# A decoder layer on one core: twelve expert slots move from the last merge and output into the samples' stage, and VectorE adds some of them there

## The chip, the cores and the metric

The kernel runs on one core of a Trainium2 chip. The metric is the device time of one execution in microseconds. Three runs gave 3580.25, 3585.42 and 3592.96, a median of 3585.42 us.

## What is computed

One layer of a decoder trunk for 1024 prompt tokens and 8 samples of one token each, all in float32:

```
xn = rmsnorm(x);  z = xn @ w_in                     # heads of three branches, and gates
merged = sig(ga)*(attention @ w_br_a) + sig(gb)*(pooling @ w_br_b) + sig(gc)*(mlstm @ w_br_c)
x = x + merged @ w_out
x = x + peer(rmsnorm(x))       # 8 heads, top 16 of 128*128 experts each
peer: sum over 8*16 experts e of  softmax_gate(e) * gelu(xn . u[e]) * v[e]
```

The samples use the same weights, with a cache of 128 keys and values, 15 rows of pooling history, and an mLSTM state of 32 matrices of 128 x 128 that is read, used and written back.

## The kernel before, in words

The prompt is eight tiles of 128 tokens. A pass handles two tiles; there are four passes (0 to 3), and the last one also carries the samples. A pass has these stages: norm (`n0`), input projection (`z`), branches (`b`), in the last pass alone the samples' own branches (`x`), merge (`m`: 24 units, each a gate product of 16 matmuls at L1105 and a branch product of 8 at L1109), output (`o`: 8 units, L1126), norm (`n1`), queries (`g`), and the experts' search (`f`, `search`, `e`).

The experts' work of each tile is cut into 128 **slots**. A slot stands for one expert of each of a tile's 128 tokens. There are 1032 of them: 8 x 128, and 8 for the samples. A slot is

- a gather of 128 rows of 8 KB (u and v beside each other) by GpSimd, L1982, into one of 8 places of a ring (place n % 8). It is issued when the place's earlier slot n-8 has been added (`free`);
- a dot product on VectorE, L1515, of the u half with x;
- a gelu (per pair of slots), a weight and a diagonal matrix on ScalarE (L1211, L1223, L1230);
- the adding of weight times the v half to the tile's sum: either on TensorE, four matmuls against the diagonal at L894, or, for the slots in `ON_DVE`, on VectorE at L1475, with no diagonal.

The slots of pass p's tiles are worked off during the stages of pass p+1 and, for the last pass, in the end of the program. `SHARES` says how many slots fall into each stage. `share_out` spreads them over the stage's **points**, named places in the program of each engine. At a point VectorE does the point's dots; TensorE adds only the slots up to the point's first, so it is one point behind. `ON_VECTOR` says which places of the ring VectorE adds itself, by stage; never the first 16 slots of a tile or its last.

The samples' stage has nine points, x0 to x8 (`sample_tensor` L431 on, `sample_scalar`, `sample_vector`). In it tile 4 ends: at x1 VectorE takes its sum out of PSUM (L1487), and TensorE may add slot 640, the first of tile 5, only after that. On VectorE the stage has small operations (L568 to L640), four rounds of the mLSTM state (`state_round`, five operations on 128 x 1024 each, L557 to L563: round 0 before x3, round 1 before x4, round 2 before x5, round 3 before x6), and the end (`c_h2`, `c_y`), which lies between x6 and x8. On TensorE, `fill` (L426, L427) brings a round's rows into PSUM: fill 0 before x3, fill 1 before x4, fill 2 before x5, fill 3 before x6. The first merge unit waits for `c_y`.

In the merge, the weights of unit k+2 (768 KB) are requested by SyncE when unit k's branch product is done (L770), since two buffers take turns; the output's (512 KB) likewise.

Of the kernel before, what the change touches and what calls it, by code (L numbers as in the profile page):

```python
# [34 lines left out]
LAST = PASSES - 1  # L35
# [27 lines left out]
RING = 8  # L63
# [10 lines left out]
def share_out():  # L74


    points = {
        "n0": [("n", 0)], "z": [("z", c, t) for c in range(NZ) for t in range(NT)],
        "b": [("b", t, i) for t in range(NT) for i in range(BRANCH_POINTS)], "x": [("x", i) for i in range(SAMPLE_POINTS)],
        "m": [("m", k, i) for k in range(3 * KC) for i in range(2)], "o": [("o", i) for i in range(NO)], "n1": [("n", 1)],  # L80
        "g": [("g", i) for i in range(3)], "f": [("f", h, i) for h in range(PH) for i in range(4)],
        "late": [("f", h, i) for h in range(2, PH) for i in range(4)],
        "search": [("e", i) for i in range(SEARCH_POINTS)], "e": [("e", i) for i in range(SEARCH_POINTS, TAIL_POINTS)],
    }
    plan = [{} for _ in range(PASSES)]
    done = 0
    for p, shares in enumerate(SHARES):
        at = done
        for stage, share in shares:
            for key in points[stage]:  # L90
                at += share / len(points[stage])
                to = 2 * round(at / 2)
                plan[p][key] = (done, to)
                done = to
    assert done == SLOTS
    return plan
# [4 lines left out]
    (("late", 40),),  # L101
# [3 lines left out]
)  # L105
SOON = (4, 4, 4, 4)
PLAN = share_out()
ON_VECTOR = {"z": (3, 7), (LAST, "z"): (1, 3, 5, 7), "b": (1, 5), "m": (1, 4, 6), (LAST, "m"): (1, 3, 5, 7), "o": tuple(range(RING)), "f": (2,)}


def vector_slots():

    own = set()
    for p, of_pass in enumerate(PLAN):
        for key, (first, last) in of_pass.items():
            for n in range(first, last):
                if n % RING in ON_VECTOR.get((p, key[0]), ON_VECTOR.get(key[0], ())) and PK <= n % P < P - 1:
                    own.add(n)
# [1969 lines left out]
```

## Time and profile before

| what | value |
|---|---|
| median of three runs | 3585.42 us |
| profiled execution, its own time | 3589.58 us |
| its span, first to last instruction | 3587.8 us |
| mean granted TensorE clock | 0.947 |
| TensorE busy | 3073.4 us (86%) |
| VectorE busy | 2324.5 us (65%) |
| ScalarE busy | 1083.9 us (30%) |
| GpSimd busy | 1216.1 us (34%) |
| moved by DMA | 1313.33 MB, mean 366 GB/s |

A time in a row is in microseconds from the span's start. A granted clock of 1.00 is 2.4 GHz, 0.50 is 1.2 GHz, and a value between is a mixture of both in that stretch. DMA share is the mean busy share of the 16 DMA engines; it can come out a little above 1. In the timeline, brackets hold the idle time before an instruction and what ended it.

### The profile page before, as it was taken

Reading aid. Unit: us, or ns where it says so; the run is one execution under the profiler, and the core shown is the slowest. Engines: PE = TensorE matmul, PEld = TensorE weight load, DVE = VectorE, ACT = ScalarE, POOL = GpSimd, SP = SyncE. Lnnn points to the kernel's source line nnn. Section 1 sums busy time; section 2 is a strip of 40 time slices with the busy share of each in tenths; the row PEclk is TensorE's granted clock in tenths of the full one; section 3 lists DMA queues with packets and bytes.
Section 4 is the critical chain, followed back from the end, with each engine's and each line's share of the span. In section 5 each row is a group of like instructions: output and inputs, shape, how many; then the busy total and the mean of one; then the engine's idle time right before and its main releaser. Section 6 shows DMA issues by size and latency. Waiting matters only on the chain.

```text
span 3587.8 us, 31309 instructions
## 1 busy us (share of the span) xinstructions
PE 3073.4 (86%) x9822; PEld 1776.0 (50%) x9822; DVE 2324.5 (65%) x5255; ACT 1083.9 (30%) x3269; POOL 1216.1 (34%) x1043
## 2 busy tenths in 40 slices
PE   7988789989987889988987989988998787777777
PEld 4667544546665544445665544443566453322222
DVE  1331678785666678885566778886667768864444
ACT  1221243442212333442222333343221234332222
POOL 0100233343343233442333333342334324444342
PEclk9999899999998999989998989997999899999999
DMA  5344899999999889999999989998999989999998
GB/s 166 102 126 140 328 386 398 382 401 364 420 420 386 352 349 421 417 372 372 417 420 401 413 349 408 390 386 318 397 420 419 404 339 401 421 420 421 422 421 354
DMA packets 206565, 1313.33 MB, mean 366 GB/s; under 512 B 27170, under 2 KB 29290, under 8 KB 73751
## 3 DMA queue, kind: packets, MB, share of 16 engines
q0 software_dynamic: 152800, 1084.63, 74.3%
q1 hardware_dynamic: 49111, 213.07, 15.5%
q10 hardware_dynamic: 4488, 13.63, 1.1%
q8 instruction: 78, 1.28, 0.1%
q14 instruction: 88, 0.72, 0.1%
HBM read 1294.81 MB, written 17.61 MB: 366 GB/s over the span
## 4 chain that ended last, share of the span: by engine, by line
PE 54%; DMA 29%; DVE 9%; ACT 4%; issue 3%; POOL 1%; ACTq 0%; DVEq 0%; POOLq 0%; SPq 0%
PE ps L894 23%; DMA arena<-uv,eidx 21%; PE ps L930 10%; PE ps L1143 5%; PE ps L1105 5%; DVE arena L1515 4%; DMA wbuf<-w_merge 4%; PE ps L1109 3%; PE ps L1126 2%; DMA wbuf<-w_o 2%; DMA xx<-xs_scr 1%; DVE xx L1475 1%; ACT wgt L1223 1%; PE ps L948 1%; PE ps L911 1%
## 5 line engine op out<-in xcount | busy, mean ns | idle before, releaser
L1982 POOL DMA_INDIRECT arena<-uv,eidx x1032 | 1200.4, 1163 | 2188.3 <-PE ps L894 1633.7
L894 PE MATMUL ps<-arena,dgs 128*128 128x512 f32 x3196 | 1542.4, 625 | 289.7 <-ACT dgs L1230 257.4
L1515 DVE CUSTOM_DVE_ANT_0 arena<-arena,xx 128x1024 f32<-128x1024 f32 x1024 | 1238.5, 1222 | 663.2 <-DMA arena<-uv,eidx 614.6
L894 PEld LDWEIGHTS ps<-arena,dgs 128*128 128x128 f32 x3196 | 614.5, 199 | 1041.8 <-issue 621.1
L1211 ACT ACTIVATE gel<-dots 128x2 f32<-128x2 f32 x516 | 104.3, 202 | 1423.4 <-DVE dots L1515 1422.7
L930 PE MATMUL ps<-wbuf,xT 128*128 128x420 f32 (+1 forms) x1152 | 426.8, 520 | 13.5 <-DMA wbuf<-w_z 12.6
L1475 DVE SCALAR_TENSOR_TENSOR xx<-arena,wgt,xx 128x1024 f32<-128x1024 f32 x225 | 288.3, 1282 | 60.1 <-ACT wgt L1223 57.5
L1105 PE MATMUL ps<-xT,wbuf 128*128 128x256 f32 (+1 forms) x1344 | 314.8, 388 | 11.9 <-DMA wbuf<-w_merge 10.1
L930 PEld LDWEIGHTS ps<-wbuf,xT 128*128 128x128 f32 (+1 forms) x1152 | 204.6, 180 | 235.6 <-issue 220.8
L1105 PEld LDWEIGHTS ps<-xT,wbuf 128*128 128x128 f32 x1344 | 258.0, 193 | 79.4 <-DMA wbuf<-w_merge 26.0
L1230 ACT ACTIVATE dgs<-cst,wgt 128x128 f32<-128x128 f32 x799 | 286.9, 396 | 15.9
L1223 ACT ACTIVATE wgt<-gates,gel 128x1 f32<-128x1 f32 x1032 | 247.7, 287 | 23.0 <-ACT gel L1211 2.6
L1143 PE MATMUL ps<-xT,wbuf 128*128 128x256 f32 (+1 forms) x1024 | 233.3, 383 | 6.3 <-issue 6.3
L1143 PEld LDWEIGHTS ps<-xT,wbuf 128*128 128x128 f32 x1024 | 195.6, 191 | 55.7 <-issue 28.8
L1109 PE MATMUL ps<-yT,wbuf 128*128 128x256 f32 (+1 forms) x768 | 182.6, 382 | 6.1 <-DMA wbuf<-w_merge 5.3
L1126 PE MATMUL ps<-wbuf,R 128*128 128x256 f32 (+1 forms) x576 | 144.8, 411 | 41.8 <-DMA wbuf<-w_o 35.5
L1109 PEld LDWEIGHTS ps<-yT,wbuf 128*128 128x128 f32 x768 | 145.2, 190 | 52.9 <-issue 26.3
L1126 PEld LDWEIGHTS ps<-wbuf,R 128*128 128x128 f32 (+1 forms) x576 | 109.5, 195 | 78.3 <-DMA wbuf<-w_o 44.3
L1766 DVE SCALAR_TENSOR_TENSOR T<-T,ps 128x256 f32<-128x256 f32 (+1 forms) x96 | 40.4, 420 | 122.2 <-PE ps L1109 121.2
L1280 ACT ACTIVATE arena<-ps 128x420 f32<-128x420 f32 x64 | 33.3, 520 | 250.3 <-PE ps L930 250.2
L911 PE MATMUL ps<-cst,R 128*128 128x128 f32 x128 | 29.3, 423 | 90.1 <-DVE R L1538 90.1
L1404 ACT ACTIVATE yT<-ps 128x256 f32<-128x256 f32 x64 | 24.4, 382 | 221.4 <-PE ps L1143 221.4
(366 smaller groups left out, 1993.1 us busy)
## 6 DMA issues: line engine op xcount, KB each, us to landing
wbuf<-w_merge SPq DMA_DIRECT2D x84, 768.0 KB, 8.5
wbuf<-w_z SPq DMA_DIRECT2D x64, 840.0 KB, 8.8
wbuf<-w_q SPq DMA_DIRECT2D x64, 512.0 KB, 7.9
arena<-uv,eidx POOLq DMA_INDIRECT x1032, 12.5
wbuf<-w_o SPq DMA_DIRECT2D x32, 512.0 KB, 7.9
xin<-x_prompt SPq DMA_DIRECT2D x8, 1024.0 KB, 11.7
wbuf<-w_merge SPq DMA_DIRECT2D x12, 512.0 KB, 8.3
grow<-gains SPq DMA_DIRECT2D x8, 512.0 KB, 9.8
```

Source lines behind the costliest of these rows:

```text
L894: done = mm(ps[:, half, :], dgs[:, j, :], ring[:, j, row_], start=(q == 0), stop=(q == P - 1), skip_group_check=True)
L930: last = mm(ps[0:rows_, 2 + 2 * (pair % 2) + t if t < NT else 6 + pair % 2, 0:ZP], xT[:, HALF * half + kc, t * P:t * P + rows_], wv[:, kc, :],
L1105: last = mm(ps[:, 2 + 2 * b, m], wv[:, c, :], xT[:, c, m], start=(c == 0), stop=(c == KC - 1))
L1109: last = mm(ps[:, 3 + 2 * b, m], wv[:, 8 + c, :], yT[:, 4 * b + c, m], start=(c == 0), stop=(c == 3))
L1126: last = mm(ps[0:rows_, 2 + 2 * (b % 2) + t if t < NT else 6 + b % 2, 0:OC], mT[:, HALF * half + c, t * P:t * P + rows_], wv[:, c, :], sta ...
L1143: last = mm(ps[:, 2 + k, m], wv[:, c, :], xT[:, c, m], start=(c == 0), stop=(c == KC - 1))
L1211: f(gel[:, j:j + 2], dots[:, j:j + 2], ACT.Gelu).then_inc(s["gelud"], 1)
L1223: last = f(wgt[:, j + i:j + i + 1], gate_of(n + i), ACT.Copy, scale=gel[:, j + i:j + i + 1])
L1230: f(dgs[:, j + i, :], ident, ACT.Copy, scale=wgt[:, j + i:j + i + 1]).then_inc(s["diagd"], 1)
L1475: v.scalar_tensor_tensor(xres, ring[:, j, D:2 * D], wgt[:, j:j + 1], xres, ALU.mult, ALU.add).then_inc(free[j], 1)
L1515: v.tensor_tensor_reduce(ring[:, j, 0:D], ring[:, j, 0:D], x, 1.0, 0.0, ALU.mult, ALU.add, dots[:, j:j + 1]).then_inc(s["dotted"], 1)
L1982: g.indirect_dma_start(ring[:, j, :], None, uv, bass.IndirectOffsetOnAxis(ap=experts, axis=0)).then_inc(got[j], 16)
```

## The change

In the last pass the samples' stage gets 36 slots where it had 24, the merge 52 where it had 60, the output 16 where it had 20. In the samples' stage VectorE adds the slots in ring places 1, 3, 5 and 7.

```diff
-    (("n0", 4), ("z", 62), ("b", 46), ("x", 24), ("m", 60), ("o", 20), ("n1", 4), ("g", 6), ("f", 46), ("search", 80), ("e", 152)),
+    (("n0", 4), ("z", 62), ("b", 46), ("x", 36), ("m", 52), ("o", 16), ("n1", 4), ("g", 6), ("f", 46), ("search", 80), ("e", 152)),
 )
-ON_VECTOR = {"z": (3, 7), (LAST, "z"): (1, 3, 5, 7), "b": (1, 5), "m": (1, 4, 6), (LAST, "m"): (1, 3, 5, 7), "o": tuple(range(RING)), "f": (2,)}
+ON_VECTOR = {"z": (3, 7), (LAST, "z"): (1, 3, 5, 7), "b": (1, 5), "m": (1, 4, 6), (LAST, "m"): (1, 3, 5, 7), "o": tuple(range(RING)), "f": (2,), "x": (1, 3, 5, 7)}
```

`share_out` turns this into the following plan. The samples' stage ran from slot 640 to 663, with 2, 4, 2, 2, 4, 2, 2, 4, 2 dots at x0 to x8; it now runs from 640 to 675 with four at every point. The merge has slots 676 to 727 (it had 664 to 723), the output 728 to 743 (724 to 743); from slot 744 on nothing changes. By place and by the rule on a tile's first 16 slots, VectorE now adds ten slots of the samples' stage: 657, 659, and so on to 675, of which 657, 659, 661 and 663 were TensorE's before. Slots 724 and 726, which VectorE added in the output, are TensorE's now. So VectorE adds 227 slots in all where it added 225.

## Rows read from the trace of the kernel before

**Rows 1.** Busy time by stage: samples, merge, output of the last pass.
```profile
core 0: us, PE busy (x) PEld busy (x) DVE busy (x) ACT busy (x) POOL busy (x), PEclk, DMA share, GB/s
2451.30:2545.90 94.60, 83.24 (x238) 37.58 (x238) 61.81 (x126) 33.76 (x86) 27.16 (x23) 0.78 0.83 302
2545.90:2739.50 193.60, 184.60 (x701) 131.69 (x699) 122.65 (x187) 40.20 (x144) 74.21 (x61) 1.00 1.01 420
2739.50:2800.90 61.40, 46.00 (x196) 29.51 (x196) 51.26 (x71) 7.19 (x31) 25.77 (x20) 0.97 1.01 419
```
**Rows 2.** The same view: the merge of pass 2, and a stretch of the end.
```profile
1634.80:1868.30 233.50, 222.94 (x788) 151.36 (x788) 131.76 (x210) 52.77 (x187) 83.78 (x74) 0.98 0.98 400
...
3300.00:3560.00 260.00, 191.94 (x417) 74.51 (x416) 127.65 (x209) 71.50 (x260) 104.46 (x104) 1.00 1.01 421
```
**Rows 3.** Costliest groups of the page: the dot and the VectorE add.
```profile
L1515 DVE CUSTOM_DVE_ANT_0 arena<-arena,xx 128x1024 f32<-128x1024 f32 x1024 | 1238.5, 1222 | 663.2 <-DMA arena<-uv,eidx 614.6
L1475 DVE SCALAR_TENSOR_TENSOR xx<-arena,wgt,xx 128x1024 f32<-128x1024 f32 x225 | 288.3, 1282 | 60.1 <-ACT wgt L1223 57.5
```
**Rows 4.** Timeline of TensorE, samples' stage: slots added, two and four at once.
```profile
2467.63 6.37 PE L894 MATMUL ps<-arena,dgs 128*128 128x512 f32 x8 [5.25 <-DVE xx L1487]
...
2477.48 10.00 PE L894 MATMUL ps<-arena,dgs 128*128 128x512 f32 x16
...
2492.11 6.08 PE L894 MATMUL ps<-arena,dgs 128*128 128x512 f32 x8
```
**Rows 5.** Timeline of VectorE, samples' stage: its waits for TensorE, in order.
```profile
2462.41 0.21 DVE L580 COPY xin<-ps 128x32 f32<-128x32 f32 x1 [7.24 <-PE ps L453]
...
2474.83 0.19 DVE L623 TENSOR_TENSOR yT<-ps,col 128x32 f32<-128x32 f32 x1 [2.67 <-PE ps L457]
...
2487.62 0.28 DVE L633 SCALAR_TENSOR_TENSOR xin<-ps,xin 64x128 f32<-64x128 f32 x1 [9.57 <-PE ps L471]
...
2492.31 1.22 DVE L557 TENSOR_TENSOR R<-arena,ps 128x1024 f32<-128x1024 f32 x1 [3.67 <-PE ps L427]
...
2503.24 1.22 DVE L557 TENSOR_TENSOR R<-arena,ps 128x1024 f32<-128x1024 f32 x1 [2.32 <-PE ps L427]
...
2524.44 1.22 DVE L557 TENSOR_TENSOR R<-R,ps 128x1024 f32<-128x1024 f32 x1 [2.79 <-issue]
```
**Rows 6.** Timeline of VectorE: the last operation before c_y is set (L678).
```profile
2539.38 0.19 DVE L678 COPY yT<-xin 128x32 f32<-128x32 f32 x1
```
**Rows 7.** Timeline of GpSimd: gathers in the samples' stage.
```profile
2471.68 1.28 POOL L1982 DMA_INDIRECT arena<-uv,eidx  x1 [12.74 <-PE ps L894]
```
**Rows 8.** Timeline of TensorE, merge: gate product, slot, branch product, a wait.
```profile
2585.35 1.88 PE L894 MATMUL ps<-arena,dgs 128*128 128x512 f32 x4
2587.07 3.72 PE L1105 MATMUL ps<-xT,wbuf 128*128 128x264 f32 x16
2590.62 1.94 PE L1109 MATMUL ps<-yT,wbuf 128*128 128x264 f32 x8
2592.41 1.88 PE L894 MATMUL ps<-arena,dgs 128*128 128x512 f32 x4
2595.38 3.83 PE L1105 MATMUL ps<-xT,wbuf 128*128 128x264 f32 x16 [1.10 <-DMA wbuf<-w_merge]
```
**Rows 9.** The weight buffers' tile in the merge, issue to landing.
```profile
DMA to landing us min/median/max: 7.7/8.6/9.9
```
**Rows 10.** Timeline of TensorE in the output: first, a later and last unit.
```profile
2739.54 5.54 PE L1126 MATMUL ps<-wbuf,R 128*128 128x256 f32 x24 [2.06 <-DVE R L1773]
...
2767.91 5.54 PE L1126 MATMUL ps<-wbuf,R 128*128 128x256 f32 x24 [2.29 <-DMA wbuf<-w_o]
...
2787.29 5.54 PE L1126 MATMUL ps<-wbuf,R 128*128 128x256 f32 x24 [0.30 <-DMA wbuf<-w_o]
```
**Rows 11.** Timeline of GpSimd in the output: a gather alone, one behind an add.
```profile
2751.12 0.94 POOL L1982 DMA_INDIRECT arena<-uv,eidx  x1 [0.30 <-issue]
2755.33 1.94 POOL L1982 DMA_INDIRECT arena<-uv,eidx  x1 [3.27 <-DVE xx L1475]
```

## The prediction, made before the changed kernel was run

> **What bounds the kernel now.** I read the busy time by stage first, for the three stages that the change touches, then the timelines of TensorE, VectorE and GpSimd in them. The reader is to see two kinds of stage. In the merge and the output the DMA engines are full (share 1.01, about 420 GB/s), TensorE is next with 184.6 of 193.6 us in the merge, and VectorE with 51.3 of 61.4 us in the output [rows 1]. In the samples' stage the DMA share is only 0.83 over 94.6 us, which is 16 us of idle DMA, and the granted clock of TensorE is 0.78 [rows 1]. Nothing is full there; GpSimd waits for TensorE to free places of the ring, once for 12.74 us [rows 7], and VectorE waits for TensorE at six places, 28 us in all [rows 5]. So it is a chain of waits between TensorE and VectorE.
>
> What a slot costs where: in the end of the program 104 gathers took 260 us with DMA at 1.01, 2.5 us each [rows 2]. A dot occupies VectorE for some 1.15 us of its pitch (1.22 with overlap) and an add for 1.28 [rows 3]. TensorE adds a slot in 1.72 us at the 2.4 GHz level (the difference between the slot's start at 2585.35 and the next product's at 2587.07, [rows 8]) and in about 3.4 at 1.2 GHz: in the two stretches of two slots the time was 6.37 and 6.08 us [rows 4].
>
> **Samples' stage: what it adds.** Twelve dots (13.8 us), ten adds (12.8 us) on VectorE, and two more slots on TensorE (26 for 24); ScalarE has a third of its time busy and is not counted. I walk the points, with the duration of rows, against the times of before.
> - x0 has four dots for two, 2.3 us. The samples' first operations on VectorE and ScalarE stand behind them. VectorE has a wait of 7.24 us there [rows 5], but ScalarE's chain behind the same dots has none, so I count the 2.3: tile 4 ends later by it, and TensorE begins slot 640 at 2470.0 instead of 2467.6.
> - x1: TensorE adds 640 to 643, not 640 and 641, before the products that VectorE waits for at L623. It stands at the low clock there; two more slots are 6.9 us. L623 comes at about 2484.7, 10 later than 2474.8.
> - x2: TensorE adds four slots, as before. They took 10.0 us with the clock rising on the way [rows 4]; begun later in the busy stretch I give them 6.9, all at 2.4 GHz. L633 then runs at 2494.5 (7 later), and round 0 at 2498.8 for 2492.3 (6.5 later). VectorE's dots here are slots 648 to 651, whose gathers need 640 to 643 freed: from 2473.7 to 2484 in my walk, landed by 2491, in time.
> - x3, x4: four slots for two each, in front of fill 1 and behind it. Two more cost 3.4 at the full clock and 6.9 at the low one, and the clock changes in this stretch. With room in VectorE's waits (2.3 and 2.8 us, [rows 5]), round 1 comes 9 us later, at 2512, and round 2 10.6 later, at 2524.
> - x5: from here TensorE has only two slots per point and VectorE leads: four dots and two adds are 4 x 1.15 + 2 x 1.28 = 7.2 us, where two dots stood (2.3). Round 3 begins at about 2537, 12.7 later. x6 and x7 lie before c_y: 14.4 us for six dots (6.9). So c_y comes near 2560 where it was at 2539.6 [rows 6], 20 later.
> - The merge began 6.3 us behind c_y, since TensorE had six slots to add first; now it has two or none. It begins near 2562 instead of 2545.9: **+16 us**.
>
> Bounds: if every added microsecond on VectorE and the two TensorE slots at the low clock lay in line, 13.8 + 12.8 + 6.9 = +33. From below, +8: if TensorE ran x1 and x3 at 2.4 GHz (3.4 and more won at each) and half of VectorE's 28 us of waits took up the work.
>
> On the adds: a gather issued alone takes GpSimd 0.94 us, one issued while VectorE adds takes 1.94 [rows 11]. Ten adds could delay gathers by 10 us in sum; but the output has 19 such adds and its DMA share is 1.01 [rows 1], so queued gathers cover it, and I count none. The Trainium skill ("SBUF — State Buffer", Who interferes with whom) speaks against the change here: a VectorE instruction with two inputs in SBUF contends with a GpSimd instruction that reads SBUF, and one blocks until the other is done. The 1.94 agrees with that; by the rule with nothing hiding it the sum below would be +7 instead of -3.
>
> **Merge: what it removes.** Eight slots: eight gathers, eight dots, four adds on VectorE, four on TensorE (28 instead of 32 up to the output). By DMA alone this is 8 x 2.5 = -20 us. The comparison with pass 2 agrees that the merge goes by its slots: 74 slots took 233.5 us and 60 took 193.6 [rows 1, 2], 2.85 us per slot. But TensorE is close behind. A unit's gate and branch product take 5.34 us (2587.07 to 2592.41, [rows 8]); 24 x 5.34 + 28 x 1.72 = 176.4 us. Then the weights: those of unit k+2 are requested when k is done and land 8.6 us later [rows 9]. In the meantime TensorE has one unit and the slots between. Before, two slots stood in every such gap, 5.34 + 3.44 = 8.8 us, just enough (a wait of 1.10 is to be seen where it wasn't, [rows 8]). In the new plan 8 of the 22 gaps have one slot, 7.1 us, so TensorE waits up to 1.5 us in each; part of this is given back in the next gap. With 4 to 5 us for that, the merge takes about 181: **-13 us**. Bounds: -20 by DMA, -7 by the four TensorE slots alone.
>
> **Output.** Four slots less. By DMA -10 us, by VectorE as much (4 x (1.15 + 1.28)). TensorE's units are chained through the weights: the eighth begins 47.8 us behind the first and ends at 53.3 [rows 10], and the last sums on VectorE follow. That cannot shrink with the slots. 61.4 becomes about 55: **-6 us**, bounds -10 and -4.
>
> Later stages keep their slots, and there each stage waits for the one before it, so the shift is carried to the end unchanged. The moved slots' DMA queue is GpSimd's alone; SyncE's reload of x behind c_y comes 20 us later, but its data is used in the output, 180 us on.
>
> **Sum.** +16 - 13 - 6 = -3 us. On the profiled execution: 3589.58 - 3 = 3586.6. The median of the runs is 4.2 lower than that execution, and I predict for it 3585.4 - 3 = **3582 us**. About 0.3% (10.8 us) is what a measurement of this kernel can tell from no change.
>
> **Rivals.**
> - *The gap is filled.* The DMA idle of 16 us in the samples' stage is used up by twelve gathers of 2.5 us, and the stage grows by only 8. For it: DMA is the resource that is full everywhere else, and total bytes don't change, so the time falls by what idle is removed, at most 16. Against it: the idle comes from places that TensorE frees late, and it now has more slots before x2. +8 - 14 - 8 = -14: 3571.
> - *The weight chain binds.* With fewer slots the merge waits for its weights in each gap, and loses only 7, the output only 4. For it: the wait in rows 8. Against it: the landing time of 8.6 is taken with DMA full, and should shorten. +16 - 7 - 4 = +5: 3590.
> - *VectorE takes the lead (slower).* From x5 on, VectorE's 7.2 us per point are in series with round 3 and c_y; TensorE idles meanwhile and falls to 1.2 GHz, so that fill 3, the slots and the start of the merge run at half pace. It decides once VectorE's chain from round 1 on has no waits left, and the start of the merge comes later than 29 us. +31 - 13 - 6 = +12: 3597. Against it: TensorE has slots to add at each point.
>
> **How the numbers follow.** The forecast gets 0.50, the filled gap 0.24, the weight chain 0.12, VectorE's lead 0.14. The forecast's own range is +-8 us, 3574 to 3590. Faster by over 0.3%: 0.19 of the filled gap and 0.04 of the forecast's edge, 0.23. Slower by over 0.3%: 0.09 of VectorE's lead, 0.03 from the edges of the others, 0.12. Between: 0.65. The range for 8 in 10 is 3569 to 3597: it takes in the filled gap at -16 and most of VectorE's lead.
>
> **What would show it.** In the profile after: the first merge product near 2562, L623 ten later, round 3 near 2537, and VectorE without waits from x5 on; DMA share of the samples' stage about 0.9; a merge of some 181 us with DMA below 1.0 and TensorE waiting for w_merge; an output of 55. It is wrong if the merge begins before 2556 or after 2570, or if the merge shrinks by the full 20.

## The result, and the profile after

Ten runs of the changed kernel gave a median of 3601.41 us (3589.85 to 3608.28), ten of the kernel before 3585.93 (3576.26 to 3593.94). The ratio is 1.0041, with a 95% interval of 1.0031 to 1.0052: 15 us slower. I had forecast 3582 us, 3 us less than before and not to be told from no change, with a range of 3569 to 3597. Ten more executions of the changed kernel gave 1.0043 [1.0028, 1.0058]; twelve more of the kernel before, against itself, 0.9997 [0.9983, 1.0012].

The first profile of the changed kernel could not show this. Its execution took 3589.85 us, the fastest of the ten, against 3589.58 for the one of before. So I took two more profiles of each. They are compared by stretches and not by their ends, since the time before the changed stage alone differs by up to 10 us between executions of one kernel: the start of L1752, the last VectorE work ahead of the samples' stage, lies at 2447.5, 2442.4 and 2451.5 in the three of before, and at 2445.9, 2442.8 and 2453.1 in the three of after.

| stretch (us) | before, three profiles | mean | after, three profiles | mean | difference |
|---|---|---|---|---|---|
| L1752 to first merge product | 98.4, 96.2, 95.5 | 96.7 | 104.5, 114.1, 113.8 | 110.8 | +14.1 |
| first merge unit | 10.5, 10.5, 10.5 | 10.5 | 20.4, 20.8, 20.9 | 20.7 | +10.2 |
| the 23 other units | 183.2, 183.7, 182.7 | 183.2 | 178.1, 177.5, 180.1 | 178.6 | -4.6 |
| output | 61.3, 61.3, 61.3 | 61.3 | 55.2, 55.3, 55.3 | 55.3 | -6.0 |
| sum | 353.4, 351.7, 349.9 | 351.7 | 358.1, 367.7, 370.2 | 365.3 | +13.7 |

Each number is a difference of two starts in the timeline: L1752, the first and second gate product (L1105) of the last pass, the first output product (L1126), and the end of the last L1794. From the last pass's second norm (L1538) to the last L1487 the three of before took 771.7, 767.0 and 769.8 us, those of after 768.9, 769.7 and 770.7. So the loss is in the three stages, as far as three profiles of each can tell. The first profile of the change is only 6 us longer than the mean of before (358.1 against 351.7), the two others 16 and 18: the stage ahead of the merge takes one of two courses, 104.5 us or 114, and the experiments come back to it.

The busy time by stage of the first profile after (samples' stage, merge, output; same columns as [rows 1]):

```profile
2449.70:2550.40 100.70, 78.59 (x244) 35.52 (x245) 78.42 (x147) 36.69 (x98) 50.14 (x31) 0.84 0.92 356
2550.40:2748.80 198.40, 181.74 (x685) 129.59 (x683) 117.31 (x181) 38.41 (x136) 61.95 (x58) 0.97 1.00 408
2748.80:2804.00 55.20, 47.45 (x196) 30.69 (x196) 40.73 (x59) 5.46 (x24) 24.08 (x16) 0.97 0.96 381
```

In this profile part of the samples' stage's idle DMA was used: its share is 0.92, where the first profile of before has 0.83. This doesn't hold for the others: the same stretch has 0.85 and 0.87 in the second and third profile of before, and 0.87 in both others of after, and 0.13 of 110 us is 14 us of idle DMA, where the three of before have 12 to 16. And the merge, with eight slots less, took 198.4 us where it took 193.6, and DMA moved 408 GB/s in it instead of 420. So idle DMA opened in the output (0.96), without being filled ahead of it in two profiles of three.

The second profile of the changed kernel, the same stages; its samples' stage is 10 us longer at a lower clock, the other two are the same:

```profile
2446.70:2556.90 110.20, 89.29 (x246) 39.56 (x245) 78.56 (x147) 36.75 (x99) 37.14 (x31) 0.76 0.87 325
2556.90:2755.20 198.30, 181.87 (x685) 129.74 (x683) 116.40 (x181) 37.97 (x136) 62.76 (x58) 0.98 1.00 408
2755.20:2810.60 55.40, 47.48 (x196) 30.66 (x196) 41.81 (x59) 5.48 (x25) 24.57 (x16) 0.97 0.96 382
```

VectorE in the samples' stage of the first profile after, the counterparts of [rows 5, 6]:

```profile
2477.29 0.19 DVE L623 TENSOR_TENSOR yT<-ps,col 128x32 f32<-128x32 f32 x1 [5.62 <-PE ps L457]
...
2490.49 1.22 DVE L557 TENSOR_TENSOR R<-arena,ps 128x1024 f32<-128x1024 f32 x1 [2.70 <-PE ps L427]
...
2501.31 1.21 DVE L557 TENSOR_TENSOR R<-arena,ps 128x1024 f32<-128x1024 f32 x1
...
2525.51 1.20 DVE L557 TENSOR_TENSOR R<-R,ps 128x1024 f32<-128x1024 f32 x1
...
2547.77 0.19 DVE L678 COPY yT<-xin 128x32 f32<-128x32 f32 x1
```

Three of the waits for TensorE are gone (before L633 and before rounds 1 and 3): in this profile VectorE leads from round 1 on. TensorE's first merge unit, with what stands around it, in the same profile:

```profile
2539.15 0.64 PE L496 MATMUL ps<-xin,ones 128*128 128x32 f32 x2 [10.35 <-DVE xin L666]
2539.60 7.45 PE L894 MATMUL ps<-arena,dgs 128*128 128x512 f32 x12
2548.58 1.98 PE L894 MATMUL ps<-arena,dgs 128*128 128x512 f32 x4 [1.53 <-ACT dgs L1230]
2550.40 3.72 PE L1105 MATMUL ps<-xT,wbuf 128*128 128x264 f32 x16
2556.31 3.24 PE L894 MATMUL ps<-arena,dgs 128*128 128x512 f32 x4 [2.18 <-ACT dgs L1230]
2562.76 3.78 PE L894 MATMUL ps<-arena,dgs 128*128 128x512 f32 x4 [3.21 <-ACT dgs L1230]
2566.34 2.35 PE L1109 MATMUL ps<-yT,wbuf 128*128 128x264 f32 x8
2568.94 1.98 PE L894 MATMUL ps<-arena,dgs 128*128 128x512 f32 x4 [0.26 <-ACT dgs L1230]
2570.76 3.72 PE L1105 MATMUL ps<-xT,wbuf 128*128 128x264 f32 x16
```

The reader is to see three things. TensorE waits 10.35 us for VectorE ahead of L496 (3.8 before). It then starts the first gate product at 2550.4, counted from L1752 only 6.1 us later than in the first profile of before. But behind that product it must add slots 672 and 674, and has to wait for both (2.18 and 3.21 us, and 0.26 for the next). TensorE's work in the unit is that of before, but after these waits it has a low clock:

```profile
2550.40:2570.80 20.40, 14.74 (x38) 7.79 (x37) 12.84 (x18) 3.53 (x13) 9.33 (x8) 0.75 1.01 416
```

A slot takes it 3.24 and 3.78 us there instead of 1.88. Of the 10 us that the unit grew, 5.7 are the waits, and most of the rest is this clock. Why the slots are late, VectorE and GpSimd show:

```profile
2550.96 1.23 DVE L1515 CUSTOM_DVE_ANT_0 arena<-arena,xx 128x1024 f32<-128x1024 f32 x1 [3.01 <-DMA arena<-uv,eidx]
...
2560.29 1.23 DVE L1515 CUSTOM_DVE_ANT_0 arena<-arena,xx 128x1024 f32<-128x1024 f32 x1 [1.30 <-DMA arena<-uv,eidx]
```

```profile
2533.85 2.82 POOL L1982 DMA_INDIRECT arena<-uv,eidx  x1 [0.66 <-DVE xx L1475]
2544.14 1.64 POOL L1982 DMA_INDIRECT arena<-uv,eidx  x1 [7.46 <-PE ps L894]
```

The first two rows are the first and the last of the four dots of point x8 (672 to 675). They begin at 2550.96, after the merge has begun, and each waits for its gather (3.01, 0.39, 1.54 and 1.30 us). In the kernel before, the last dot of x8 was done at 2541.9, before TensorE began the merge at 2545.9:

```profile
2540.63 1.22 DVE L1515 CUSTOM_DVE_ANT_0 arena<-arena,xx 128x1024 f32<-128x1024 f32 x1
```

The gather of slot 672, at 2544.14, is issued after GpSimd had no free place for 7.46 us, and the places came free only when TensorE had left L496. The samples' stage of the new plan does not end where the merge begins: its last point spills over into the first unit.

### The profile page after: what moved, and what is told of

The parts are those of the page before. It is cut to its first block, busy times and chain, and to the rows that moved or that the text cites. A ratio compares the mean times of both kernels' runs of the same rounds, so it can differ in the third digit from the quotient of the medians.

```text
span 3588.1 us, 31293 instructions
## 1 busy us (share of the span) xinstructions
PE 3061.1 (85%) x9814; PEld 1768.2 (49%) x9814; DVE 2324.4 (65%) x5257; ACT 1082.7 (30%) x3267; POOL 1222.3 (34%) x1043
## 4 chain that ended last, share of the span: by engine, by line
PE 56%; DMA 27%; DVE 9%; ACT 4%; issue 3%; POOL 1%; SPq 0%; DVEq 0%; ACTq 0%; POOLq 0%
PE ps L894 23%; DMA arena<-uv,eidx 18%; PE ps L930 11%; PE ps L1105 6%; PE ps L1143 5%; DMA wbuf<-w_merge 5%; DVE arena L1515 4%; PE ps L1109 3%; PE ps L1126 3%; DMA wbuf<-w_o 3%; DMA xx<-xs_scr 1%; DVE xx L1475 1%; PE ps L948 1%; ACT wgt L1223 1%; PE ps L911 1%
## 5 line engine op out<-in xcount | busy, mean ns | idle before, releaser
L1105 PE MATMUL ps<-xT,wbuf 128*128 128x256 f32 (+1 forms) x1344 | 314.3, 388 | 15.9 <-DMA wbuf<-w_merge 14.3
L1105 PEld LDWEIGHTS ps<-xT,wbuf 128*128 128x128 f32 x1344 | 256.7, 193 | 81.9 <-DMA wbuf<-w_merge 31.7
L1109 PE MATMUL ps<-yT,wbuf 128*128 128x256 f32 (+1 forms) x768 | 183.2, 383 | 5.4 <-DMA wbuf<-w_merge 4.6
L1126 PE MATMUL ps<-wbuf,R 128*128 128x256 f32 (+1 forms) x576 | 146.1, 414 | 41.8 <-DMA wbuf<-w_o 35.5
L1126 PEld LDWEIGHTS ps<-wbuf,R 128*128 128x128 f32 (+1 forms) x576 | 110.7, 197 | 78.4 <-DMA wbuf<-w_o 43.2
L1388 ACT ACTIVATE T<-ps 128x256 f32<-128x256 f32 (+1 forms) x84 | 32.0, 381 | 267.7 <-PE ps L1105 267.5
```

The lines of the kernel that those rows point to most:

```text
L1105: last = mm(ps[:, 2 + 2 * b, m], wv[:, c, :], xT[:, c, m], start=(c == 0), stop=(c == KC - 1))
L1109: last = mm(ps[:, 3 + 2 * b, m], wv[:, 8 + c, :], yT[:, 4 * b + c, m], start=(c == 0), stop=(c == 3))
L1126: last = mm(ps[0:rows_, 2 + 2 * (b % 2) + t if t < NT else 6 + b % 2, 0:OC], mT[:, HALF * half + c, t * P:t * P + rows_], wv[:, c, :], sta ...
```

## The experiments

Stretches are as in the table above, from each kernel's own profile; "stage + unit 1" is from L1752 to the second unit's gate product, 106.0 to 108.8 in the kernel before and 124.9, 134.9 and 134.7 in the changed one.

**The changed kernel and the kernel before, once more.**

> The changed kernel once more, for a second profile: the first profiled execution (3589.85 us) was the fastest of ten and sits 11.6 below their median, so it can't show where the 15 us are. Theory A (the moved slots cost more in the samples' stage and the merge's first unit than merge and output give back): ratio 1.003 to 1.005, and this profile, if near 3600, has its first output matmul 15 to 20 us later than the kernel before, not 9. Theory B (the loss lies behind the output, in the search or the last tiles): first output matmul again about 9 later, and the rest of the difference after it.

> The kernel before once more, unchanged, for a second profile and as a measure of what no change looks like: ratio 1.000 within 0.002; merge 193 us and output 61 us again, and the samples' stage 94 to 96 us.

Measured: 1.0043 [1.0028, 1.0058] and 0.9997 [0.9983, 1.0012]. In the second profile of the change the first output product lies 312.4 us behind L1752, where it is 292.0 and 290.4 in the first two of before: 21 later, of which the output gives 6 back. Theory A holds, B falls.

**The shares alone.**

```diff
-... ("x", 24), ("m", 60), ("o", 20) ...
+... ("x", 36), ("m", 52), ("o", 16) ...      # no "x" in ON_VECTOR
```

> The new shares alone (36, 52, 16), no adds on VectorE in the samples' stage; TensorE adds all 36. Theory A: as slow as the change or slower, 1.003 to 1.008, since ten more slots on TensorE at 1.7 to 3.4 us make the stage 15 to 30 us longer than before. Theory C (the VectorE adds are what costs, in line with round 3 and c_y and against GpSimd's issues): no slower than before, 0.998 to 1.001.

Measured: 1.0047 [1.0030, 1.0064], median 3602.01 us. Stage + unit 1 took 123.7 us (unit 1 15.6), the 23 units 177.9, the output 58.1. The shares alone cost all of it. TensorE's wait at L496 was 3.09 us in this profile, not 10: without the adds on VectorE that wait is gone and the time is no better.

**The adds on VectorE alone.**

```diff
-ON_VECTOR = {... "f": (2,)}
+ON_VECTOR = {... "f": (2,), "x": (1, 3, 5, 7)}      # shares (24, 60, 20)
```

> The adds on VectorE alone: shares as before (24, 60, 20), slots 657, 659, 661 and 663 added by VectorE instead of TensorE. Theory A: the same within 0.002 or a little faster (four slots of 1.7 us less on TensorE in front of the merge, -3 to -6 us). Theory C: slower, 1.001 to 1.003, since four adds of 1.28 us lie in front of round 3 and c_y.

Measured: 0.9993 [0.9979, 1.0008]. No difference: with these shares only four slots (657, 659, 661, 663) move to VectorE, and they neither cost nor help. For the ten of the change it is the run before this one that tells: 1.0047 without them, 1.0043 with them. Theory C falls by both. In this profile stage + unit 1 took 103.3 us, 4 less than before, and the 23 other units 186.4, 3 more.

**Half of the bytes for the stage's gathers.**

```diff
-  g.indirect_dma_start(ring[:, j, :], None, uv, ...)
+  small = 640 <= n < 676
+  out, table = (ring[:, j, 0:D], uv.rearrange("n (a d) -> (n a) d", a=2)) if small else (ring[:, j, :], uv)
+  g.indirect_dma_start(out, None, table, ...)
```

> The changed kernel, with the gathers of the samples' stage's 36 slots (640 to 675) cut to half their bytes: 128 rows of 4 KB from the table's rows read as 1024 wide, so these slots' products are of other data, and the v half in the ring is that of an earlier slot. Everything else is as in the change. Theory D (the samples' stage with 36 slots, and the first merge unit behind it, go at the pace of the gathers): 28 gathers lie in the stage at 2.5 us each, half of that is 35 us of DMA less; the first merge unit falls from 20.5 to about 11 us and the stretch from the stage's start to the second unit's gate product by 12 us or more. Theory E (TensorE and VectorE in turn are the pace: fills, rounds, slots in order): the stretch shortens by less than 5 us.

Measured: 1.0030 [1.0015, 1.0045]. In its one profile stage + unit 1 took 130.7 us, between the changed kernel's 124.9 and 134.9; unit 1 alone 17.3 for 20.7. The stage in this profile, its start cut off by 20 us:

```profile
2467.30:2560.80 93.50, 80.16 (x207) 34.37 (x208) 69.07 (x109) 23.33 (x73) 34.96 (x29) 0.75 0.56 181
```

DMA is at 0.56 there and the stage is as long as in the second and third profile of the change. So the bytes are not its pace: theory D falls for the stage, and explains 3 of the 10 us of unit 1. What is left is theory E, that TensorE and VectorE set it in turn.

**The merge's slots alone.** Shares (24, 52, 28).

> Shares (24, 52, 28): the samples' stage as before the change, the merge as in the change, its eight slots given to the output, no VectorE adds in the samples' stage. It measures what eight slots less bring in the merge alone. By my prediction's step the merge shrinks by 13 us (first unit's gate product to the output), the output grows by 8 x 2.5 = 20: ratio 1.002. Theory F (TensorE and the weights' landing are a floor right under the merge of before): the merge shrinks by 5 or 6 only, output +20: ratio 1.004.

Measured: 1.0052 [1.0037, 1.0068]. The samples' stage is that of before (stage + unit 1: 106.6 us). The merge and the output:

```profile
2542.80:2730.80 188.00, 177.56 (x686) 128.81 (x684) 107.74 (x168) 35.56 (x128) 54.59 (x53) 1.00 0.99 402
2730.80:2810.80 80.00, 47.42 (x196) 30.64 (x196) 69.47 (x95) 9.56 (x42) 39.64 (x28) 0.85 0.97 397
```

Eight slots less take 193.7 to 188.0, 5.7 us, at 402 GB/s. The output pays 18.7 for its eight. Unit 1 took 10.5 us, so its 20 us in the change come with the longer samples' stage.

**Half the step.** Shares (30, 56, 18), VectorE adds.

> Half the step: (30, 56, 18) with VectorE adds in the samples' stage. If every moved slot costs the same, ratio 1.002. Theory D: the idle DMA of the stage takes the first slots for nothing and the cost begins once it is used up: 1.000 to 1.001.

Measured: 1.0018 [1.0005, 1.0031]. Stage + unit 1 took 116.5 us (9 more than the mean of before), unit 1 17.4, the 23 units 182.5, the output 58.3. That is the ratio of an equal price per slot, 1.002. Its interval still takes in the 1.001 of theory D, but the 9 us in the profile speak against free room for six slots. Whether the first one or two would be free is not shown.

**All twelve from the merge.** Shares (36, 48, 20), VectorE adds.

> All twelve slots taken from the merge: (36, 48, 20), VectorE adds as in the change. Theory F (merge floor): the merge gives back no more than in the change and the output not at all, so 6 us slower than the change: 1.006. If the merge gave 2 us per slot, as my prediction's 13 for 8 has it, the ratio would be that of the change, 1.004.

Measured: 1.0093 [1.0070, 1.0116], far outside both. Not only does the merge give nothing back, it got longer: 192.8 us for the 23 units, where 52 slots took 178.6 and 60 took 183.2. TensorE in it, two units in a row:

```profile
2641.74 3.83 PE L1105 MATMUL ps<-xT,wbuf 128*128 128x264 f32 x16 [1.35 <-DMA wbuf<-w_merge]
2645.40 1.88 PE L894 MATMUL ps<-arena,dgs 128*128 128x512 f32 x4
2647.12 1.94 PE L1109 MATMUL ps<-yT,wbuf 128*128 128x264 f32 x8
2650.07 3.83 PE L1105 MATMUL ps<-xT,wbuf 128*128 128x264 f32 x16 [1.01 <-DMA wbuf<-w_merge]
```

In this plan every gap between a unit's branch product and the gate product two units on holds one slot: 5.34 + 1.72 = 7.06 us of TensorE, and the weights land 8.6 us after they are asked for (median in this merge too).

It is the place of the slots, and not their number alone. Here TensorE's one slot of a unit always stands between its gate and its branch product, so that a gap holds only the one of the unit in it. With 52 slots most units have one as well, but in many of them it stands behind the branch product, and then a gap holds two. Both kinds can be seen in the first profile of the change:

```profile
2686.49 3.72 PE L1105 MATMUL ps<-xT,wbuf 128*128 128x264 f32 x16
2690.05 1.94 PE L1109 MATMUL ps<-yT,wbuf 128*128 128x264 f32 x8
2691.83 1.88 PE L894 MATMUL ps<-arena,dgs 128*128 128x512 f32 x4
2693.55 3.78 PE L1105 MATMUL ps<-xT,wbuf 128*128 128x264 f32 x16
...
2711.28 1.88 PE L894 MATMUL ps<-arena,dgs 128*128 128x512 f32 x4
2712.99 1.94 PE L1109 MATMUL ps<-yT,wbuf 128*128 128x264 f32 x8
2716.42 3.83 PE L1105 MATMUL ps<-xT,wbuf 128*128 128x264 f32 x16 [1.49 <-DMA wbuf<-w_merge]
```

In the three profiles of the change, leaving out the first unit and the thirteenth, which has two slots, a unit took 7.3 us where the gap ahead of the next gate product holds two slots and 8.2 where it holds one. The 48 slots with each one behind its branch product were not run.

**The same with small weights.** Shares (36, 48, 20); in the last pass's merge a third of the weights.

```diff
-  part=lambda i: (2 / 3 if p == 0 and i < EARLY else 0, 1))
+  part=lambda i: (2 / 3 if p == 0 and i < EARLY else 0, 1 / 3 if p == LAST else 1))
```

> Shares (36, 48, 20) with VectorE adds, and in the last pass's merge only the first 512 of each unit's 1536 weight columns are loaded (256 KB for 768 KB), so most of the products there use old weights. With all weights the 23 units behind the first took 192.8 us with 48 slots, more than with 52 (178.0) or 60 (183.2). Theory F (chain of branch product, request and landing of the weights): landing gets shorter, and the 23 units fall to TensorE's own 23 x 7.06 = 162 to 168 us. If it were VectorE or ScalarE in turn with TensorE that made 48 slots slower, they stay above 185.

Measured, one execution (3594.99 us): the 23 units took 164.8 us instead of 192.8, and the landing fell to a median of 5.6 us, below 7.06.

```profile
2584.20:2749.00 164.80, 162.99 (x645) 121.99 (x643) 97.43 (x156) 33.70 (x115) 43.39 (x47) 1.00 0.92 347
```

```profile
DMA to landing us min/median/max: 4.5/5.6/8.0
```

TensorE is busy for 163.0 of 164.8 us. Theory F is shown: with 48 slots the chain of branch product, request, landing and gate product is the merge's floor, and what a slot less brings depends on how many are left in each gap.

**The dots of x6 behind c_h2.**

```diff
-            point(LAST, "x", 6)
             done(f"c_cqr{ROUNDS - 1}")
...
             v.tensor_tensor(hq, hh, hh, ALU.mult).then_inc(s["smp_v"], SMP["v"].step("c_h2"))
+            point(LAST, "x", 6)
```

> The changed kernel with one move on VectorE: the four dots and two adds of point x6 stand behind the operations that end in c_h2 (L659 to L666) instead of ahead of them. In the change TensorE waits 10.35 us for c_h2 there, frees no places meanwhile, and the gathers that the first merge unit needs are issued that much later. Theory G (this wait makes the late gathers and with them the first merge unit's 20 us): the wait at L496 falls to 3 us or less, the first unit from 20 to 14 or less, c_y to second unit's product 6 us or more shorter, and the ratio from 1.004 to 1.002. Theory H (four slots per point keep DMA, VectorE and TensorE all busy to the end of the stage, the wait is only where the slack collects): the time moves to other waits, the ratio stays at 1.004.

> The same move in the kernel before (shares 24, 60, 20). TensorE waits 3.8 us for c_h2 there. Theory G: 2 to 4 us faster than before, ratio 0.999; Theory H: 1.000.

Measured: 1.0028 [1.0017, 1.0039] in the changed kernel, 1.0014 [1.0001, 1.0028] in the kernel before. TensorE's wait there fell as foreseen,

```profile
2546.04 0.41 PE L496 MATMUL ps<-xin,ones 128*128 128x32 f32 x2 [2.88 <-DVE xin L665]
2550.72 6.02 PE L894 MATMUL ps<-arena,dgs 128*128 128x512 f32 x8 [4.26 <-ACT dgs L1230]
2558.21 1.98 PE L894 MATMUL ps<-arena,dgs 128*128 128x512 f32 x4 [1.47 <-ACT dgs L1230]
2561.64 1.98 PE L894 MATMUL ps<-arena,dgs 128*128 128x512 f32 x4 [1.45 <-ACT dgs L1230]
```

but most of it came back in the next three waits, for the diagonals of slots whose dots are now later. From L496 to the first gate product TensorE waited 10.1 us, where it was 11.9 and 10.8 in the first two profiles of the change. Unit 1 took 18.2 us for 20.7, and from c_y to the second unit's product it was 20.7 us for 22.8 to 23.3, not the 6 less of theory G. The ratio lies 0.0015 below the change's, with intervals that overlap, between the expectations of G and H. So the wait is not the whole cause, and that it is a part of it is likely but not shown; the shares alone cost as much with a wait of 3.09 us. In the kernel before the move is no gain; the interval lies just above 1.

**The other direction.** Shares (20, 62, 22), no VectorE adds.

> The other direction: shares (20, 62, 22), no VectorE adds in the samples' stage. Four slots leave that stage. DMA is full in merge and output of the kernel before, so four slots cost 10 us there by the gathers; by the measured prices of the change (stage and first unit +16 to +26 for twelve) the stage gives back 5 to 8. Ratio 1.001, 0.999 to 1.002; below 0.998 would mean that the kernel before already has too many slots in the stage.

Measured: 0.9999 [0.9986, 1.0012]. Stage + unit 1 took 102.1 us, 5 less; the 23 units 186.3, the output 66.6, together 8 more. No version of the study is shown to be faster than the kernel before.

**Three matmuls in TensorE's gap.** In x0, ahead of the wait for tile 4's end:

```diff
+            for _ in range(3):
+                mm(ps[:, 7, :], ident, cst[:, 0:512], start=True, stop=True)
             point(LAST, "x", 1)
```

> The changed kernel with three more matmuls (128 x 512, constants into a PSUM bank that is free) on TensorE behind the samples' small products of x0, where it waits for tile 4's end (7.0 us in the second profile of the change). The profiles of the change are of two kinds: in one each group of four slots takes 7.13 us and the stage up to the first merge product 104.5 us, in the other the groups take 9.2 to 10.1 and the stage 114.1. Theory K (the granted clock in this stage, set by what TensorE did in the gap, decides between the two, and most executions of the change are of the long kind): groups of 7.1 to 7.5 us from x2 on, stage about 104, and a ratio against the kernel before of 1.001 to 1.002 instead of 1.004. If the ratio stays at 1.004 with the groups at 7.1, the two kinds are not what makes the median.

> The same three matmuls in the kernel before. Its groups have two or four slots and its two profiles end the stage at 98.4 and 96.2 us. Theory K: 0 to 3 us faster, ratio 0.999 to 1.000.

> A third look at the changed kernel. Theory K: of the long kind (groups of 9 to 10 us, stage 114), like the second; if it is of the short kind, the typical execution of the change isn't the long one.

> A third look at the kernel before: stage 96 to 99 us, first merge unit 10.5, the 23 others 183, output 61.

The third profile of the changed kernel was of the long kind (113.8 us to the first merge product, 3610.97 us in all); that of the kernel before gave 95.5. TensorE's groups of four slots (x16) in the first profile of the change, then in the third:

```profile
2467.15 9.31 PE L894 MATMUL ps<-arena,dgs 128*128 128x512 f32 x16 [6.66 <-DVE xx L1487]
2479.48 7.13 PE L894 MATMUL ps<-arena,dgs 128*128 128x512 f32 x16
2490.28 7.13 PE L894 MATMUL ps<-arena,dgs 128*128 128x512 f32 x16
2500.97 7.13 PE L894 MATMUL ps<-arena,dgs 128*128 128x512 f32 x16
```

```profile
2473.89 9.87 PE L894 MATMUL ps<-arena,dgs 128*128 128x512 f32 x16 [6.79 <-DVE xx L1487]
2487.19 10.04 PE L894 MATMUL ps<-arena,dgs 128*128 128x512 f32 x16
2501.82 9.55 PE L894 MATMUL ps<-arena,dgs 128*128 128x512 f32 x16
2516.24 9.18 PE L894 MATMUL ps<-arena,dgs 128*128 128x512 f32 x16
```

With the three matmuls (one profile) the groups took 8.65, 7.13, 8.83 and 9.51 us and the stage 107.9; the ratio was 1.0044 [1.0027, 1.0060]. In the kernel before it was 1.0006 [0.9992, 1.0021]. So the clock rose sooner and was lost again behind x2, and no gain in time can be told: the groups of 7.1 to 7.5 us that theory K asked for did not come. Whether holding it would bring the change near 1.002 stays open: this test didn't hold it.

## Why the prediction was wrong

- **What bounds the kernel: right in kind.** The samples' stage is a chain of TensorE and VectorE; with the gathers' bytes halved it was as long as in two of the change's three profiles.
- **Samples' stage, +16: right in size and, as a mean, in its walk** (+14.1; +7.8 and +17 by kind). Taken as means of the three profiles and counted from L1752, round 0 came 6.7 us later than before, round 1 9.8, round 2 11.0, round 3 11.1 and c_y 18.3; I had 6.5, 9, 10.6, 12.7 and 20. The steps inside were rougher: L623 came 5.3 later and not 10. The pairs of profiles scatter widely around this walk, so that it fits so well is in part luck. The first profile of before is of another course than its second and third (rounds 0 to 3 at 44.8, 55.7, 66.1 and 76.9 us, against 39.3, 49.0, 60.7 and 74.1 in the second), and the change has two courses as well (44.6, 55.4, 67.0 and 79.6 in its first, 49.2, 63.6, 76.6 and 89.2 in its second). Held against each other, the two first profiles would put nearly all the growth behind round 2. That an execution can take either course I had not foreseen. I had called the forecast wrong if the merge began before 2556. In the first profile it did (2550.4), in the others not (2556.9 and 2566.9); a time counted from the span's start is a poor sign, since the stages ahead of it differ by up to 10 us.
- **VectorE's adds, counted at nothing against GpSimd: right.** The shares without the ten adds were no faster than with them (1.0047 and 1.0043), so the case of +7 us did not come. A single gather issued beside VectorE's work took 4.62 us in the first profile after. But I had read too much out of one row of 1.94 us: between 2440 and 2860 us in the first profile of before, the 60 gathers that began beside a dot alone have a median of 0.97 us, the 8 beside an add alone 1.64.
- **Merge, -13: the step that failed.** The merge became 5.6 us longer (+10.2 - 4.6). Two things were wrong in it. First, the 23 later units gave 4.6 and not 13. I had named the chain through the weights, and even counted its eight short gaps rightly, but priced its waits at 4 to 5 us in sum, on top of 176.4 us of TensorE's own work (the terms give 176.3; nothing hangs on it). Measured in the 23 later units of the first profile after, TensorE waited 8.9 us for weights at nine places and 11 us in all (it was busy for 167.0 of 178.0); in the kernel before it was 4.3 us for weights and 9 in all. With 52 slots in the merge of (24, 52, 28), where nothing else is changed ahead of it, the whole merge shrank by 5.7, about my bound of 7. The gather rate, by which I had put the other bound at -20, and the 2.85 us per slot from pass 2 don't count once a gap is shorter than the landing: with one slot in each gap (48 slots) the units got longer than with 60 slots and two in each gap. Second, I let the merge begin with "two slots or none" to add and counted it as free from there. The dots of x8 come after TensorE has begun the merge, and unit 1 takes 20.7 us for 10.5. This was a cost of the samples' stage, behind its end as I had drawn it. How those 10 us divide among their causes is open: half of the gathers' bytes gave 3 back, the moved dots 2.5, each in one profile.
- **Output, -6: right** (-6.0).
- **Later stages carry the shift: right**, to 0.3 us in the means (769.5 before, 769.8 after).
- **The rivals.** The gap filled: its DMA part happened in one profile (0.92), not in the two others (0.87), and brought no gain. The weight chain: its merge term (-7) is near the measured ones (-4.6 for the later units, -5.7 where the merge alone was changed), its reason is the one shown by the small weights. VectorE's lead: seen in the first profile after, in the wait of 10 us at L496 and the low clock of unit 1. The sum by measured terms is 14.1 + 10.2 - 4.6 - 6.0 = 13.7, and the runs say 15. Ahead of the second unit 24 us were lost, where VectorE's lead had 31 to the start of the merge. I had given each its own case and let each keep the forecast's other terms.

## What to carry to other kernels

Idle DMA in a stage of waits is not room: what is moved there goes at the pace of the engines that wait for each other, and a full stage that it leaves gets shorter only down to its next floor. Before crediting a stage with the work taken out of it, look for the loop of request and landing right under the present bound, and count what stands in each of its gaps, by place and not only by number; here the plan with the fewest slots made the stage longer. Take several profiles of a kernel before reading a difference of a few microseconds off a pair of them. And follow the last moved items past the stage's end, to the instruction that has to wait for them.

## What the runs showed of the hardware

- Landing of a weight tile against its size, in the same stage: 768 KB 8.6 us, 256 KB 5.6 us (medians), though DMA was 0.92 busy in both.
- The granted clock of TensorE in a stage of short groups and gaps took two courses in executions of the same kernel: groups of four slots at 7.13 us each behind the first, or at 9.2 to 10.1, with a mean clock of 0.84 and 0.76 in the stage, and 9 to 10 us between them. Of the seven profiles that have this stage's slots and adds (the change's three, and those with half the bytes, with the moved dots, and with 48 slots in the merge), two are of the short kind.
- The kernel before has two courses as well: its group of four slots at x2 took 10.0 us in the first profile and 7.13 in the other two, the next one, at x4, 7.13 and 9.2. They end the stage 2 to 3 us apart (98.4 against 96.2 and 95.5).
